# The feed-forward of an encoder layer moved into a phase of its own and computed by one level of Strassen's scheme

## The chip, the cores and the metric

The kernel runs on one core of a Trainium2 chip. Its engines are TensorE (PE, matrix products, with its weight loads listed as PEld), VectorE (DVE), ScalarE (ACT), GpSimd (POOL) and SyncE (SP); SP, ACT and POOL issue the DMAs. The metric is the time of one execution on the device in microseconds (us), the median of several; lower is better.

## What is computed

One layer of a hybrid streaming encoder over 2096 columns (16 meta tokens, 2048 prompt frames, 32 frames of a running stream) of width 1024, all in float32. The change touches the last two lines:

```python
proj = rmsnorm(x) @ w_in                         # 1024 -> 4096: x_a, x_b, g_a, g_b
merged = sig(g_a) * (rglru(conv4(x_a)) @ w_br_a) + sig(g_b) * (pool(x_b) @ w_br_b)
x = x + merged @ w_out                           # "x1" below
g, u = split(rmsnorm(x) @ w_gu)                  # 1024 -> 2 * 2816
y = rmsnorm(x + (silu(g) * u) @ w_down)          # 2816 -> 1024, then the final norm
```

## The kernel before

Data lie with the 1024 features on partitions, in KT = 8 tiles of 128, and frames along the free dimension. The frames go through in NB = 5 blocks of 416 columns (432 in block 0). Every float32 product is made of three passes: each operand is split into a rounded part (hi) and the rest (lo), and `product` (L403 to L406) issues hi x hi, hi x lo and lo x hi, so that one 128x128 piece of weights against one tile of data is three matmuls of 416 columns.

A block runs through the mixer and then the feed-forward. `pe_order` lists the mixer as jobs of 24 matmuls (8 tiles x 3): `xa` (8 jobs), then four rounds p of gates (12 matmuls from the small ring `sring`) with `ga` and `gb` jobs, then `a`, `xb`, two more `gb`, `b` and `o` (x1 = x + o). In block 0 four `fuse` steps of 24 matmuls with 512 columns stand between `xa` jobs. The feed-forward has 22 tiles of hidden features in 11 pairs: for each pair two `g` and two `u` jobs (96 matmuls) and then `dn` (8 outputs x 2 x 3 = 48 matmuls), one pair behind; in all (96 + 48) x 11 = 1584 matmuls a block.

Weights stream from HBM: SP loads 512 KB (1024 columns) into one of RAW = 3 slots `wraw`, ACT writes the hi part into a slot of `wring` (`split_hi`, L553), DVE the lo part (`split_lo`, L1131), and PE uses the slot for one job. The ring has RING = 4 slots. Each engine's order is written out by hand: the calls named `ahead` put ACT's split four slots and DVE's split three slots ahead of the job beside which they stand. PE writes job n into PSUM bank n mod 8, and the reader of the bank (ACT or DVE) frees it.

In the feed-forward DVE and ACT handle each hidden tile in `hidden` (L1101, L744, L748: scale by the norm, Silu, times u, hi and lo parts) and DVE adds each `dn` output to `main` (`add_down`, L1122). The square sums, norm and scaling of the next block's input (`square`, `square_sum`, `invert`, `normalize`) also lie in the feed-forward. In the mixer rounds ACT runs sigmoid, tanh, exp and sqrt, and DVE the scan (`heads`). GpSimd copies small state columns and issues the loads of x and the stores of y. The end of the program (L440 to L450, L1285 to L1291) is a last norm done with small matmuls, eight scalings and the stores.

Of the kernel before, what the change touches and what calls it, by code (L numbers as in the profile page):

```python
# [5 lines left out]
P = 128  # L6
# [3 lines left out]
NB = 5  # L10
# [5 lines left out]
COLS = 2096  # L16
W = 432
# [5 lines left out]
PART = (0, 128, 256, LW - P)  # L23
# [20 lines left out]
def pe_order(b):  # L44
# [14 lines left out]
    for p in range(4 if b else 0):  # L59
        if p == 3:  # L60
            out.append(("n3", b - 1, 0))
# [3 lines left out]
    out += [("xb", b, k) for k in range(KT)]  # L65
# [3 lines left out]
    for i in range(PAIRS + 1):  # L69
        if i < PAIRS:  # L70
            for j in range(2):
                out += [("g", b, 2 * i + j), ("u", b, 2 * i + j)]
                if i == j == 0:
                    out.append(("n2", b, 0))
        if i:
            out += [("dn", b, (i - 1) * KT + m) for m in range(KT)]
        if i == 4 and b < NB - 1:
            out.append(("n1", b + 1, 0))
    if b == NB - 1:
        out.append(("n3", b, 0))  # L80
# [3 lines left out]
ORDER = [name for b in range(NB) for name in pe_order(b)]  # L84
JOB = {name: n for n, name in enumerate(ORDER)}


def slot_order():


    out = []
    for s, b, i in ORDER:
        if s == "dn" and i % 4 == 0:
            out.append(("d", b, i // 4))
        elif s == "w" and i % 4 == 0:
# [33 lines left out]
def side_before():  # L129
# [22 lines left out]
def build(nc, dx, dwm, dws, dcst, dfix, dst0, dy, dst, fused):  # L152
# [4 lines left out]
    MUL, ADD, SUB = ALU.mult, ALU.add, ALU.subtract  # L157
    ctx = ExitStack()
# [1197 lines left out]
```

## Time and profile before

| | before |
|---|---|
| median of 3 runs | 2878.49 us (2877.73 to 2879.58) |
| span of the profiled execution, first to last instruction | 2875.3 us |
| PE busy | 2853.1 us, 15028 matmuls |
| PEld busy | 2821.2 us |
| DVE busy | 1941.4 us, 2843 instructions |
| ACT busy | 1257.3 us, 1762 instructions |
| POOL busy | 98.5 us |
| DMA | 354.5 MB, 123 GB/s |
| mean granted clock of TensorE | 0.998 of full |

Busy is the time in which an engine works on some instruction. Matmuls are pipelined, so the busy time of PE says only that it was fed; how fast it goes is read from the distance between starts. The chain that ended last is the list of work, followed back from the last instruction, in which each piece waits for the one before it.

### The profile page before, as it was taken

Reading aid. Unit: us, or ns where it says so; the run is one execution under the profiler, and the core shown is the slowest. Engines: PE = TensorE matmul, PEld = TensorE weight load, DVE = VectorE, ACT = ScalarE, POOL = GpSimd, SP = SyncE. Lnnn points to the kernel's source line nnn. Section 1 sums busy time; section 2 is a strip of 40 time slices with the busy share of each in tenths; the row PEclk is TensorE's granted clock in tenths of the full one; section 3 lists DMA queues with packets and bytes.
Section 4 is the critical chain, followed back from the end, with each engine's and each line's share of the span. In section 5 each row is a group of like instructions: output and inputs, shape, how many; then the busy total and the mean of one; then the engine's idle time right before and its main releaser. Section 6 shows DMA issues by size and latency. Waiting matters only on the chain.

```text
span 2875.3 us, 37697 instructions
## 1 busy us (share of the span) xinstructions
PE 2853.1 (99%) x15028; PEld 2821.2 (98%) x15028; DVE 1941.4 (68%) x2843; ACT 1257.3 (44%) x1762; POOL 98.5 (3%) x188
## 2 busy tenths in 40 slices
PE   8999999999999999999999999999999999999998
PEld 7999999999999999999999999999999999999998
DVE  7867667677666675776666767766666586766565
ACT  6733434258333433573333336634333275343222
POOL 2000000010000000200000001000000010000000
PEclk9999999999999999999999999999999999999999
DMA  7333333333443333243433332433333324333332
GB/s 244 121 125 126 133 117 111 124 110 110 144 137 124 110 121 117 102 137 134 138 117 117 115 118 102 141 128 127 118 124 117 110 100 146 116 110 125 117 118 78
DMA packets 108188, 354.50 MB, mean 123 GB/s; under 512 B 12144, under 2 KB 22768, under 8 KB 108016
## 3 DMA queue, kind: packets, MB, share of 16 engines
q1 hardware_dynamic: 102624, 336.21, 33.7%
q0 software_dynamic: 4096, 13.64, 1.4%
q8 instruction: 120, 1.97, 0.3%
q10 hardware_dynamic: 1296, 2.26, 0.2%
q14 instruction: 52, 0.43, 0.0%
HBM read 339.19 MB, written 12.87 MB: 122 GB/s over the span
## 4 chain that ended last, share of the span: by engine, by line
PE 98%; DMA 1%; DVE 1%; ACT 0%; issue 0%; SPq 0%; DVEq 0%; ACTq 0%
PE ps L405 97%; DMA wraw<-dwm 1%; SPq L279 0%; DVE gb L941 0%; DMA xres<-dx 0%; DVE main L1291 0%; ACT wring L553 0%; PE ps L432 0%; DVE wring L1131 0%; PE ps L433 0%; ACT sring L559 0%; PE ps L450 0%; DVE ylo L946 0%; ACT main L664 0%; DVE sring L1135 0%
## 5 line engine op out<-in xcount | busy, mean ns | idle before, releaser
L405 PE MATMUL ps<-yhi,wring 128*128 128x416 f32 x4800 | 1309.0, 351 | 0.0
L1131 DVE TENSOR_TENSOR wring<-wraw,wring 128x1024 fp32r<-128x1024 f32 x610 | 746.0, 1224 | 302.2 <-ACT wring L553 301.0
L405 PEld LDWEIGHTS ps<-yhi,wring 128*128 128x128 f32 x4800 | 900.7, 188 | 6.8
L405 PE MATMUL ps<-xhi,wring 128*128 128x416 f32 (+1 forms) x3200 | 875.2, 353 | 8.5 <-DVE wring L1131 8.5
L553 ACT ACTIVATE wring<-wraw 128x1024 fp32r<-128x1024 f32 x610 | 641.0, 1051 | 465.5 <-PE ps L405 460.7
L405 PE MATMUL ps<-ylo,wring 128*128 128x416 f32 x2400 | 841.1, 350 | 0.0
L405 PEld LDWEIGHTS ps<-xhi,wring 128*128 128x128 f32 x3200 | 602.2, 188 | 15.0 <-issue 8.5
L405 PE MATMUL ps<-xlo,wring 128*128 128x416 f32 (+1 forms) x1600 | 562.7, 352 | 0.0
L405 PE MATMUL ps<-hhi,wring 128*128 128x416 f32 x1760 | 485.0, 352 | 0.0
L405 PEld LDWEIGHTS ps<-ylo,wring 128*128 128x128 f32 x2400 | 452.2, 188 | 3.7
L405 PEld LDWEIGHTS ps<-hhi,wring 128*128 128x128 f32 x1760 | 329.3, 188 | 2.4
L405 PE MATMUL ps<-hlo,wring 128*128 128x416 f32 x880 | 307.8, 350 | 0.0
L405 PEld LDWEIGHTS ps<-xlo,wring 128*128 128x128 f32 x1600 | 302.2, 189 | 3.4
L1122 DVE TENSOR_TENSOR main<-ps,main 128x416 f32<-128x416 f32 x440 | 239.7, 585 | 28.7 <-PE ps L405 27.5
L744 ACT ACTIVATE tmp<-tmp 128x416 f32<-128x416 f32 x110 | 60.7, 551 | 310.7 <-DVE tmp L1107 310.7
L748 ACT ACTIVATE hhi<-tmp 128x416 fp32r<-128x416 f32 x110 | 60.7, 552 | 308.6 <-DVE tmp L1113 308.6
L405 PEld LDWEIGHTS ps<-hlo,wring 128*128 128x128 f32 x880 | 165.3, 188 | 2.5
L1107 DVE TENSOR_TENSOR tmp<-ps,rstd_n 128x416 f32<-128x416 f32 x110 | 64.7, 588 | 93.2 <-PE ps L405 93.0
L1115 DVE TENSOR_TENSOR hlo<-tmp,hhi 128x416 fp32r<-128x416 f32 x110 | 65.1, 592 | 67.9 <-ACT hhi L748 67.9
L1113 DVE TENSOR_TENSOR tmp<-ps,tmp 128x416 f32<-128x416 f32 x110 | 65.2, 593 | 49.6 <-PE ps L405 47.9
L941 DVE SCALAR_TENSOR_TENSOR gb<-tbuf,cst,gb 128x416 f32<-128x416 f32 (+3 forms) x144 | 80.2, 583 | 9.2 <-ACT gb L608 5.1
L838 ACT ACTIVATE xhi<-ga 128x416 fp32r<-128x416 f32 x40 | 22.1, 552 | 124.2 <-DVE ga L1241 124.2
(171 smaller groups left out, 1603.8 us busy)
## 6 DMA issues: line engine op xcount, KB each, us to landing
wraw<-dwm SPq DMA_DIRECT2D x577, 512.0 KB, 3.2
wraw<-fused SPq DMA_DIRECT2D x40, 512.0 KB, 3.2
xres<-dx POOLq DMA_DIRECT2D x32, 208.0 KB, 3.0
dy<-main POOLq DMA_DIRECT2D x32, 208.0 KB, 2.2
sraw<-dws SPq DMA_DIRECT2D x24, 256.0 KB, 4.3
fused<-main SPq DMA_DIRECT2D x16, 256.0 KB, 4.1
xres<-dx SPq DMA_DIRECT2D x4, 216.0 KB, 5.4
xres<-dx ACTq DMA_DIRECT2D x4, 216.0 KB, 5.8
```

What stands on the lines that cost most here:

```text
L405: mm = nc.tensor.matmul(out, wt[:, c * P:(c + 1) * P], x, start=(first and q == 0), stop=(last and q == 2))
L553: A(wring[:, n % RING, 0, :], wraw[:, n % RAW, :], ACT.Copy, scale=cst[:, PSC, i:i + 1] if s == "w" else 1.0).then_inc(w_hi, 1)
L744: A(tmp[:, f % 2, 0:LW], tmp[:, f % 2, 0:LW], ACT.Silu).then_inc(silu, 1)
L748: A(hhi[:, f % 4, 0:LW], tmp[:, 2 + f % 2, 0:LW], ACT.Copy).then_inc(h_hi, 1)
L838: A(xhi[:, m, live(b)], ga[:, m, :], ACT.Copy).then_inc(m_hi, 1)
L941: V.scalar_tensor_tensor(gb[:, h, c:c + n], t[:, o + v:o + v + n], cst[:, CW0 + v, h:h + 1], gb[:, h, c:c + n], MUL, ADD).then_inc(tap, 1)
L1107: V.tensor_tensor(t, bank(("g", b, f))[:, 0:LW], rstd[1][:, 0:LW], MUL).then_inc(drained[JOB[("g", b, f)] % 8], 1)
L1113: V.tensor_tensor(h, bank(("u", b, f))[:, 0:LW], t, MUL).then_inc(drained[JOB[("u", b, f)] % 8], 1)
L1115: V.tensor_tensor(hlo[:, f % 4, 0:LW], h, hhi[:, f % 4, 0:LW].bitcast(f32), SUB).then_inc(h_lo, 1)
L1122: V.tensor_tensor(main[:, m, :], bank(name)[:, 0:LW], main[:, m, :], ADD).then_inc(drained[JOB[name] % 8], 1)
L1131: V.tensor_tensor(wring[:, n % RING, 1, :], wraw[:, n % RAW, :], wring[:, n % RING, 0, :].bitcast(f32), SUB).then_inc(w_lo, 1)
```

## The change

The five blocks now run the mixer alone, one after the other. Each leaves x1 in HBM (`x1s`) and, once its norm is known, the normed and scaled y = x1 * rstd * g2 (`ys`, in `make_y`). Then the feed-forward runs as a phase of its own over NT = 3 steps s of 2 x 348 or 2 x 346 columns.

A product of (1024 -> n) on two column halves is cut into 2 x 2 blocks of features and columns, and the Winograd form of Strassen's scheme makes it of 7 half-size products instead of 8. Sums of weight blocks are made on the chip: 34 pieces of weights (4 x 512 columns) are loaded by GpSimd, summed in place by four DVE additions each (`prepare`) and stored in HBM, during blocks 1 to 4. Sums of data blocks are made by three GpSimd subtractions for each of four tile pairs (`operand`), split into hi and lo by ACT and DVE (`operand_hi`, `operand_lo`), before each step s. Partial products that several outputs share are chained in PSUM: two banks (a pair, for gate and up, or for two output tiles) are held through several products, and what has built up is read out in between (`tap_out` by ACT, `add_out` and `add_down` by DVE). A hidden pair p is `gate_up(s, p)`: 7 products k of 24 matmuls, of 348 or 346 columns. `down(s, g)` takes two pairs at once (the last group one): 14 half products hh of 12 matmuls (6 in the last group), each read out by one `add_down` of 2 x 348 columns. The steps are gu0, gu1, gu2, dn0, gu3, gu4, dn1 ... gu9, gu10, dn4, dn5.

To make room the ring has 3 slots (`RING`), so each `ahead` of the same place now handles a slot one earlier. The norm of the next block moves into the stages `a`, `xb` and `o`. The final norm of step s runs in gu0 to gu2 of step s + 1; that of the last step at the end, with a full-width reciprocal in place of the small matmuls.

In the core of the diff below stand, in this order, constants, TensorE's `gate_up`, the sixth product in VectorE's `gate_up`, its `add_down` and `prepare`, and GpSimd's first subtraction in `operand`.

```diff
-RING = 4
+RING = 3
+NT = 3
+TH = (348, 346, 346)
+PROD = (1, 5, 6, 3, 7, 2, 4)
+ROLE = {1: 0, 6: 0, 7: 0, 4: 0, 5: 1, 3: 1, 2: 2}
+REBUILD = {2: 0, 3: 1, 5: 2, 6: 3}
...
+            def gate_up(s, p):
+                for k, prod in enumerate(PROD):
+                    wh, wl = weights(SLOT[("gu", s, p, k)])
...
+                    hold(("gu", s, p, 0, k, 0))
+                    for v in range(2):
+                        out = bank(("gu", s, p, 0, k, v))[:, 0:TH[s]]
+                        for j in range(4):
+                            mm = product(out, wh, wl, 4 * v + j, ycomb[:, c, 0, j, 0:TH[s]], ycomb[:, c, 1, j, 0:TH[s]],
+                                         j == 0 and prod in OPENS, j == 3 and prod in ENDS, True)
+                        mm.then_inc(ready, 1)
...
+                    elif k == 5:
+                        add_out(s, p, 5, 0, 0)
+                        dve.wait_ge(*clear(gu(s, p, 5)))
+                        dve.wait_ge(silu3, n + 1)
+                        V.tensor_tensor(work[:, 7:10, 0:w], work[:, 7:10, 0:w], work[:, 0:3, 0:w], MUL).then_inc(h_mult, 1)
...
+            def add_down(s, g, hh):
...
+                done(name)
...
+                V.tensor_tensor(out, both(name, w), out, ADD).then_inc(cleared[BANK[name] // 2], 1)
...
+            def prepare(b, c):
...
+                V.tensor_tensor(q3, q2, q3, ADD).then_inc(prep_step, 1)
+                dve.wait_ge(prep_step, 4 * i + 1)
+                V.tensor_tensor(q2, q0, q2, SUB).then_inc(prep_step, 1)
+                V.tensor_tensor(q0, q3, q0, SUB).then_inc(prep_step, 1)
+                dve.wait_ge(prep_step, 4 * i + 3)
+                V.tensor_tensor(q1, q1, q0, SUB).then_inc(prep_step, 1)
...
+                if j:
+                    pool.wait_ge(a_lo, 4 * n)
+                nc.gpsimd.tensor_tensor(work[:, 3:5, 0:w], work[:, b0 + 1:b0 + 3, 0:w], work[:, b0:b0 + 2, 0:w], SUB).then_inc(y_diff, 1)
```

The first place is VectorE at the end of a hidden pair and the start of the down products. Before, the pair's last tile is followed by two groups of four additions of one bank (`main<-ps`):

```order
L1110 TENSOR_TENSOR tmp<-tmp,rstd_n 128x416 [waits silu]
L1113 TENSOR_TENSOR tmp<-ps,tmp 128x416 [waits ready,sr_done]
L1115 TENSOR_TENSOR hlo<-tmp,hhi 128x416 [waits h_hi]
L1131 TENSOR_TENSOR wring<-wraw,wring 128x1024 [waits w_hi]
L1122 TENSOR_TENSOR main<-ps,main 128x416 [waits ready] x4
```

Now this stands there, in step 0 from product k = 5 of pair 2 on to the first two additions of dn0 (`xacc<-ps`):

```order
L1503 TENSOR_TENSOR work<-ps,work 128x2x348 [waits cleared0,ready]
L1545 TENSOR_TENSOR work<-work 128x1044 [waits silu3,cleared2]
L1547 TENSOR_TENSOR work<-work 128x696 [waits h_mult]
L1549 TENSOR_TENSOR work<-work 128x348 [waits h_diff]
L1590 TENSOR_TENSOR wring<-wraw,wring 128x1024 [waits w_hi]
L1551 TENSOR_TENSOR hcomb<-work,hcomb 128x696 [waits h_hi]
L1555 TENSOR_TENSOR work<-ps,work 128x348 [waits cleared0,ready]
L1558 TENSOR_TENSOR work<-work 128x348 [waits h_diff,cleared0]
L1560 TENSOR_TENSOR hcomb<-work,hcomb 128x1044 [waits h_hi]
...
L1563 TENSOR_TENSOR hcomb<-work,hcomb 128x348 [waits h_hi]
L1565 TENSOR_TENSOR hcomb<-work,hcomb 128x348 [waits h_hi]
L1579 TENSOR_TENSOR xacc<-ps,xacc 128x2x348 [waits x1_in,ready]
```

The whole work of a pair (three products' worth of hidden data) comes after its sixth and seventh product, and the additions of dn come behind it. On TensorE the products of that place wait for pairs of banks. `cleared0` to `cleared3` are the four pairs; the last two products of pair 2 and the first three of dn0 are:

```order
L635 MATMUL ps<-ycomb,wring 128x348 [waits cleared2,w_lo]
L635 MATMUL ps<-ycomb,wring 128x348 x23
L635 MATMUL ps<-ycomb,wring 128x348 [waits cleared0,w_lo]
L635 MATMUL ps<-ycomb,wring 128x348 x23
L635 MATMUL ps<-hcomb,wring 128x348 [waits w_lo,cleared3,h_lo,h_hi]
L635 MATMUL ps<-hcomb,wring 128x348 x11
L635 MATMUL ps<-hcomb,wring 128x348 [waits cleared0,w_lo]
L635 MATMUL ps<-hcomb,wring 128x348 x11
L635 MATMUL ps<-hcomb,wring 128x348 [waits cleared3,w_lo]
```

Before, a dn job stood in one of eight banks in turn, six matmuls each. Now the second half product of dn takes the pair that the seventh product of the hidden pair has just left (cleared by L1555), and the third adds onto what the first left (read by the first L1579).

The third place is ScalarE in dn4, where the data sums of the next step are split (`ycomb<-work`, the waits `y_diff` are for GpSimd's subtractions) between the weight splits (`wring<-wraw`) of the running products:

```order
L795 ACTIVATE wring<-wraw 128x1024 [waits ready,raw_in1]
L1004 ACTIVATE ycomb<-work 128x2x346 [waits y_in0,ready]
L1005 ACTIVATE ycomb<-work 128x346
L1007 ACTIVATE ycomb<-work 128x3x346 [waits y_diff]
L1009 ACTIVATE ycomb<-work 128x346 [waits y_diff]
L795 ACTIVATE wring<-wraw 128x1024 [waits ready,raw_in2]
L1004 ACTIVATE ycomb<-work 128x2x346 [waits y_in1,ready]
```

Before, nothing of the kind stood in the feed-forward; ScalarE had there, for each hidden tile:

```order
L744 ACTIVATE tmp<-tmp 128x416 [waits drained4]
L553 ACTIVATE wring<-wraw 128x1024 [waits ready,raw_in1]
L748 ACTIVATE hhi<-tmp 128x416 [waits drained5]
L553 ACTIVATE wring<-wraw 128x1024 [waits ready,raw_in2]
```

## Rows read from the trace of the kernel before

**Rows 1.** The page: busy time of the engines, and the chain by engine.
```profile
PE 2853.1 (99%) x15028; PEld 2821.2 (98%) x15028; DVE 1941.4 (68%) x2843; ACT 1257.3 (44%) x1762; POOL 98.5 (3%) x188
PE 98%; DMA 1%; DVE 1%; ACT 0%; issue 0%; SPq 0%; DVEq 0%; ACTq 0%
```

**Rows 2.** Waits of PE, the longest: us in total, times, longest.
```profile
PE ps L405 <- DVE wring L1131: 8.5, 1, 8.5
```

**Rows 3.** The chain in order of time: start us, us, what; two steady stretches.
```profile
315.19 118.03 PE ps L405 x624
694.93 183.88 PE ps L405 x972
```

**Rows 4.** Timeline of PE: start us, us, line, operation, shapes, count.
```profile
45.39 4.28 PE L405 MATMUL ps<-wring,sring 128*128 128x512 f32 x18
...
51.98 0.56 PE L405 MATMUL ps<-xhi,wring 128*128 128x432 f32 x2
...
55.50 0.55 PE L405 MATMUL ps<-xhi,wring 128*128 128x432 f32 x2
...
2863.29 0.35 PE L445 MATMUL ps<-ones,tot 128*128 128x2 f32 x2 [1.36 <-ACT sq L577]
2863.51 0.36 PE L446 MATMUL ps<-ones,sq 128*128 128x2 f32 x2
```

**Rows 5.** Timeline of PE, last matmul, and DVE and ACT behind it.
```profile
2861.58 0.35 PE L405 MATMUL ps<-hhi,wring 128*128 128x416 f32 x1
2861.97 0.59 DVE L1122 TENSOR_TENSOR main<-ps,main 128x416 f32<-128x416 f32 x1
...
2862.60 0.55 ACT L577 ACTIVATE sq<-main 128x416 f32<-128x416 f32 x1 [0.58 <-DVE main L1122]
```

**Rows 6.** Groups by form: busy us, mean ns of one | idle before, releaser.
```profile
L1131 DVE TENSOR_TENSOR wring<-wraw,wring 128x1024 fp32r<-128x1024 f32 x610 | 746.0, 1224 | 302.2 <-ACT wring L553 301.0
L553 ACT ACTIVATE wring<-wraw 128x1024 fp32r<-128x1024 f32 x610 | 641.0, 1051 | 465.5 <-PE ps L405 460.7 <-DMA wraw<-dwm 4.7
...
L1122 DVE TENSOR_TENSOR main<-ps,main 128x416 f32<-128x416 f32 x440 | 239.7, 585 | 28.7 <-PE ps L405 27.5
...
L744 ACT ACTIVATE tmp<-tmp 128x416 f32<-128x416 f32 x110 | 60.7, 551 | 310.7 <-DVE tmp L1107 310.7
...
L901 DVE RECIPROCAL rstd_n<-rstd_n 128x416 f32<-128x416 f32 x13 | 35.7, 2750 | 36.1 <-ACT rstd_n L587 36.1
```

**Rows 7.** Timeline of DVE at the start of block 0: weight splits, square sums between.
```profile
12.80 2.37 DVE L1131 TENSOR_TENSOR wring<-wraw,wring 128x1024 fp32r<-128x1024 f32 x2
...
21.59 2.47 DVE L1128 SCALAR_TENSOR_TENSOR wring<-wraw,cst,wring 128x1024 fp32r<-128x1024 f32 x2
```

**Rows 8.** Timeline of block 1's rounds: first gates on PE, two splits on DVE.
```profile
642.21 0.35 PE L405 MATMUL ps<-yhi,sring 128*128 128x416 f32 x1
...
654.16 1.22 DVE L1131 TENSOR_TENSOR wring<-wraw,wring 128x1024 fp32r<-128x1024 f32 x1
...
676.55 1.22 DVE L1131 TENSOR_TENSOR wring<-wraw,wring 128x1024 fp32r<-128x1024 f32 x1
```

**Rows 9.** Windows: stretch, us, busy PE PEld DVE ACT POOL, clock, DMA share, GB/s.
```profile
305.70:605.90 300.20, 300.20 (x1590) 297.69 (x1589) 192.87 (x266) 106.99 (x136) 1.61 (x3) 1.00 0.33 117
...
642.00:715.40 73.40, 73.40 (x390) 72.85 (x389) 52.93 (x79) 65.71 (x98) 0.19 (x1) 1.00 0.31 104
```

**Rows 10.** Timeline of PE at the one long wait of block 0.
```profile
84.28 0.73 PE L405 MATMUL ps<-yhi,sring 128*128 128x432 f32 x1 [2.76 <-ACT tmp L676]
84.81 0.56 PE L405 MATMUL ps<-ylo,sring 128*128 128x432 f32 x1
```

**Rows 11.** Windows, columns as in rows 9: the same place.
```profile
84.00:88.00 4.00, 3.72 (x12) 3.54 (x13) 1.60 (x3) 4.00 (x9) 0.00 (x0) 0.59 0.00 0
```

**Rows 12.** Timeline of POOL: subtractions and products on 8 columns, early and later.
```profile
14.17 1.06 POOL L332 TENSOR_TENSOR lac<-lac 128x8 f32<-128x8 f32 x1
...
27.52 0.20 POOL L341 TENSOR_TENSOR lac<-lac 128x8 f32<-128x8 f32 x1
```

**Rows 13.** DMA issues: KB each, median us from issue to landing.
```profile
xres<-dx POOLq DMA_DIRECT2D x32, 208.0 KB, 3.0
```

More of the change, by code:

```diff
@@ L64, in pe_order @@
     out += [("a", b, m) for m in range(KT)]
-    out += [("xb", b, k) for k in range(KT)]
+    for k in range(KT):
+        out.append(("xb", b, k))
+        if k == 1 and b < NB - 1:
+            out.append(("n1", b + 1, 0))
     out += [("gb", b, 6), ("gb", b, 7)]
@@ L398, in free, with hold, product, full @@
             def free(name):
-                n = JOB[name]
-                if n >= 8:
-                    pe.wait_ge(drained[n % 8], n // 8)
-            def product(out, wh, wl, c, xh, xl, first, last):
+                if len(name) == 3 and NEED[name]:
+                    pe.wait_ge(drained[BANK[name]], NEED[name])
+            def hold(name):
+                if NEED[name]:
+                    pe.wait_ge(cleared[BANK[name] // 2], NEED[name])
+                else:
+                    for q in range(2):
+                        pe.wait_ge(drained[BANK[name] + q], MIXED[BANK[name] + q])
+            def product(out, wh, wl, c, xh, xl, first, last, chain=False):
                 for q, (wt, x) in enumerate(((wh, xh), (wh, xl), (wl, xh))):
-                    mm = nc.tensor.matmul(out, wt[:, c * P:(c + 1) * P], x, start=(first and q == 0), stop=(last and q == 2))
+                    mm = nc.tensor.matmul(out, wt[:, c * P:(c + 1) * P], x, start=(first and q == 0), stop=(last and q == 2), skip_group_check=chain)
                 return mm
-            def full(name, xh, xl, before=()):
+            def full(name, xh, xl, before=(), cols=None):
                 s, b, i = name
@@ L418, in full, with column_sum @@
                 mm.then_inc(ready, 1)
[L420 to L423 removed]
+            def column_sum(name):
+                kind, b, _ = name
+                if name == ("n1", 0, 0):
                     pe.wait_ge(sq_summed, sq_index(kind, b, 7) + 1)
                     free(name)
[L426 removed]
+                    nc.tensor.matmul(bank(name)[:, 0:W], ones[:].bitcast(f32), tot[:, 0:W], start=True, stop=True).then_inc(ready, 1)
@@ new lines, in down @@
+            def down(s, g):
+                n, width = s * PAIRS + GROUPS[g][-1] + 1, len(GROUPS[g])
+                pe.wait_ge(h_hi, 4 * n)
+                pe.wait_ge(h_lo, 4 * n)
+                for hh in range(14):
+                    mp, k = divmod(hh, 7)
+                    wh, wl = weights(SLOT[("dn", s, g, hh // 2)])
+                    c = COMBO[PROD[k]]
+                    hold(("dn", s, g, mp, k, 0))
+                    for v in range(2):
+                        out = bank(("dn", s, g, mp, k, v))[:, 0:TH[s]]
+                        for t, p in enumerate(GROUPS[g]):
+                            mm = product(out, wh, wl, 2 * width * (hh % 2) + width * v + t, hcomb[:, p % 3, 0, c, 0:TH[s]],
+                                         hcomb[:, p % 3, 1, c, 0:TH[s]], t == 0 and PROD[k] in OPENS, t == width - 1 and PROD[k] in ENDS, True)
+                        mm.then_inc(ready, 1)
```

986 lines of the change are left out of this document (661 added, 325 removed).

## The prediction

> **What bounds the kernel now.** I read the page first: PE is busy 99% of the span and 98% of the chain is PE [rows 1]. Then the waits: the longest of PE is 8.5 us, once, at the start [rows 2]. So nothing but TensorE sets the time, and every other engine is cover. The chain in order of time says how fast PE goes: 624 matmuls in 118.03 us and 972 in 183.88 us, 189.2 ns from start to start at 416 columns [rows 3]. The timeline gives the same for other widths: six times three matmuls of 432 columns from 51.98 to 55.50 are 195.6 ns each, and 18 of 512 columns in 4.28 us, less 0.36 to 0.40 for the last one's own length, are 228 to 231 ns [rows 4]. That is a slope of about 0.41 ns a column and some 19 ns that do not shrink. Two matmuls of 2 columns with their weight loads start 0.22 us after the two before, 110 ns each [rows 4]. So loading weights does not hold the rate at 346 columns either, and fewer columns do pay.
>
> **The products.** Before, 1584 matmuls x 5 blocks = 7920 x 189.2 ns = 1498.5 us; the window over one feed-forward has 300.2 us for it [rows 9]. After, each step s has 11 x 168 (gate and up) + 84 x 11 (down) = 2772 matmuls. At 0.41 ns a column the one step of 348 columns has 161.3 ns, the two of 346 have 160.5 ns: 2772 x 161.3 + 5544 x 160.5 = 1337 us. **Gain 161 us**, not the 187 us (an eighth) that the count of columns gives, since 396 more matmuls each carry the fixed part. Column sums change by less than 1 us.
>
> The fixed part is where a page can be weighed. In the Trainium skill, "TensorE: Matmul & The Clock Gate", Part 2, the gap between matmuls is N/2.4 + 2.5 ns at full clock. By that 416 columns are 175.8 ns, 13 ns below the rows, and the gain would be 7920 x 175.8 - 8316 x about 147 = 170 us; I keep the rows.
>
> **What the cover must now do, a hidden pair.** Seven products of 24 matmuls are 3.86 us each, 27.0 us a pair. VectorE has 0.585 us at 416 and 1.224 at 1024 columns [rows 6], so 0.51, 0.88 and 1.25 us at 348, 696 and 1044; a second one behind an independent first comes 0.09 earlier (two splits in 2.37) [rows 7]. ScalarE has 0.55 and 1.05 us at 416 and 1024 [rows 6]. A matmul's end is 0.35 us after its start, 0.16 later than the next could start, and an engine that waits starts 0.04 after it [rows 5]. A pair's sum on VectorE (7 splits, 3 additions of two banks, and the hidden work) is 18 us of 27: enough. The order is what matters. From the end R of the sixth product's slot: 0.16 + 0.04, addition of two banks 0.88, Silu on 1044 columns 1.1, product 1.29, differences 0.92 and 0.55, split 1.13, lo part 0.79, seventh product's multiply 0.42 = 7.3 us. The pair of banks that this last step frees is wanted again at R + 7.7 where another hidden pair follows: 0.35 us of slack, no wait (18 places). Two-bank and strided forms are in no row; priced as one wide one at the low end, and 0.1 more each at the high end.
>
> **Hidden pair to down.** Where dn follows, the half products are 1.93 us, and that bank pair is wanted at R + 3.86 + 1.93 = 5.8: PE waits 1.6. The third half product adds onto the first, so it needs VectorE's first addition, and that stands behind difference, lo part, split and two more lo parts and itself: 7.3 + 4.5 = 11.8 us after R, wanted at 7.7. PE comes out **4.1 us late**, and nothing gives it back. 15 such places; 13 plain ones cost 53 us. Behind that the additions (2 x 0.79 + 1.13 = 2.7 us in 3.86) keep up. In dn5 (6 matmuls, 0.96 us) they don't: 2 x 0.79 + 0.6 = 2.2 us against 1.93 a slot, 2 us each time; the first dn of steps 1 and 2 also waits for the residual, loaded only after the y stores of gu2: 1 to 2 us each. One dn5 and both of these are 5 us (two dn5 stand below).
>
> **Rebuilding the data sums.** In dn4 of steps 0 and 1 four operands go one after another through a load (3.0 us to land [rows 13]), three subtractions on POOL, the hi parts on ACT, the lo parts on DVE (each waits for the former's lo parts), and ACT's and DVE's weight splits and additions are queued behind these waits. POOL on hundreds of columns is in no row. On 8 columns it takes 0.20 us, and 1.06 where DVE is at work [rows 12]; with VectorE's slope on top, an operand is 2.0 us at the low end, and 6.1 us with contention and a doubled slope. Walking the order with these, dn5 begins its third half product 14 to 24 us late; I take 18 (DVE is busy 7 tenths of the time, nearer the contended row): 36 us for both, the 4.1 inside. The same chain in the last `o` stage, four operands in 36 us with the last one started at the sixth job, makes the first hidden pair 7 us late (5 to 10).
>
> The Trainium skill, "SBUF — State Buffer", § SBUF: two separate sides, says that GpSimd and VectorE instructions with two SBUF inputs lock each other out for a whole instruction. That agrees with 1.06 against 0.20, and it would make VectorE wait too; it is a rival below.
>
> **The ring of 3.** In the rounds of block 1 gates start at 642.2 [rows 8], so with 2.27 us for gates and 4.54 a job gb0 starts at 653.5. The split at 654.16 is for the slot one earlier now, gb0's: done at 655.4, 1.9 us late. The one at 676.55 serves gb2, wanted at 674.0: 1.8 more. The other splits of the rounds end before they are wanted on the delayed schedule. 3.7 x 4 = 15 us. The sums of weights (34 x 2.75 us on DVE) lie in its idle time: it is busy 52.9 of 73.4 us there [rows 9], and they come after the splits; if a load is late they cost up to 10 us. In block 0 the split at 21.59 [rows 7] is now slot 2, wanted at 19.6: 3.2 us late; the fuse steps, two slots each out of three, and the first quad add some 7: 10 us (3 to 20).
>
> **The end.** Before, the last matmul ends at 2861.9 and the span at 2875.3: 13.4 us. Now: last addition 0.9, six sums of squares of 0.93, split 1.7, sums 1.3, root 0.8, a reciprocal of 692 columns (2.75 us at 416 [rows 6]) 4.6, eight scalings 6.9, store 2.1 = 24; with three sums in dn5: +12.
>
> **The clock.** After a wait of 2.76 us matmuls of 432 columns come 0.36 us apart instead of 0.195, and the granted clock is 0.59 over those 4 us: 1.2 GHz for ten matmuls, 1.65 us lost [rows 10, 11]. Waits of 1.4 us cost nothing of the kind. The 2.6 us at each dn are near the former; I take half of 15 x 1.65 = 12 us, from 0 to 25.
>
> **Sum**: -161 + 53 + 36 + 5 + 7 + 15 + 10 + 12 + 12 = -11. The profiled span of 2875.3 becomes 2864, and the median lies 3.2 above the span: **2867 us**, 0.4% faster: nine tenths of the gain is given back. Its own range is 2835 to 2900.
>
> **Rivals.**
> *The tails are covered.* If the additions of dn come in time, the 53 and 12 go, and half of the 36: 2867 - 83 = 2784. For it: VectorE's sum is far below PE's. Against: the order of the instructions, in which no addition can pass the hidden work.
> *The slack of 0.35 us is none.* A chain of nine steps over three engines, four of them in forms that no row shows; with 0.15 us more for each, 1.0 us is lost at 18 places between hidden pairs and 1.3 more at 15 dn, 38 us, and the clock falls at most of them (+30): 2935. It decides from 0.35 us on; this is the case slower than before. Against it: all hand-offs in the rows are 0.04 us.
> *The lock.* If VectorE waits for GpSimd as well, twelve subtractions of 1.3 us stop it in each rebuild and at the entry, some 8 us each on the path: 2891. By the skill's rule named above.
> *It doesn't do what it says*: PE held by weight loads would leave 8316 x 189.2, 75 us more; rows 4 exclude it.
>
> **Chances.** Forecast 0.5 (of that 0.28 under 2872.7, 0.12 within 0.2%, 0.10 above), tails covered 0.27, no slack 0.18, lock 0.05. What a measurement can tell is about 0.2%, 5.8 us. Faster 0.55, same 0.13, slower 0.32. The range reaches from the covered case to most of the slower one: 2780 to 2925.
>
> **What would show it.** On the chain steady PE stretches at 160 to 161 ns in the hidden pairs; in PE's waits some 15 times 1.6 and 2.6 us for VectorE (`work<-ps`, `xacc<-ps`); two larger heaps at dn5 for ACT or DVE; granted clock below 1 at dn. A share of PE waits below 40 us, or waits between hidden pairs, makes the forecast wrong.

## The result

| | before | after |
|---|---|---|
| median | 2878.11 us (2877.53 to 2879.58) | 2899.27 us (2897.45 to 2899.66) |
| profiled span | 2875.3 us | 2897.4 us |
| PE busy, matmuls | 2853.1 us, 15028 | 2720.9 us, 15404 |
| DVE busy | 1941.4 us | 2104.6 us |
| DMA | 354.5 MB, 123 GB/s | 481.87 MB, 166 GB/s |
| granted clock of TensorE | 0.998 | 0.981 |

The changed kernel is **slower by 0.73%** (ratio 1.0073, interval 1.0059 to 1.0088). The forecast was 2867 us, 0.4% faster. The time lies just inside the range given for that sum (2835 to 2900); the direction is the other one.

The page, busy time and the chain by engine, as in [rows 1]:

```profile
PE 2720.9 (94%) x15404; PEld 2676.2 (92%) x15404; DVE 2104.6 (73%) x2784; ACT 1367.3 (47%) x1849; POOL 250.6 (9%) x425
PE 67%; DVE 15%; ACT 7%; issue 5%; DMA 2%; POOL 2%; SPq 0%; DVEq 0%; ACTq 0%; POOLq 0%
```

PE's waits (us in total, times, longest); before, only the one of 8.5 us was longer than 3 us [rows 2]:

```profile
PE ps L635 <- DVE xacc L1579: 65.8, 33, 5.3
PE ps L635 <- DVE work L1555: 33.6, 19, 3.2
PE ps L635 <- DVE wring L1590: 30.2, 21, 8.7
PE ps L635 <- issue: 14.0, 1, 14.0
PE ps L673 <- issue: 8.5, 1, 8.5
PE ps L635 <- DVE xlo L1256: 5.2, 4, 1.3
```

PE is busy for 132 us less and waits instead, mostly for VectorE: PE's share of the chain falls from 98% to 67%. Between the first and the last instruction 154 us more are idle than before (2897.4 - 2720.9 against 2875.3 - 2853.1).

The windows show where (stretch, us, then busy time with counts of PE, PEld, DVE, ACT, POOL, clock, DMA share, GB/s). The first two are two hidden pairs of step 0 and of step 1, 336 matmuls each. The next two are dn4 with dn5 in steps 0 and 1, where the data operands are rebuilt, and the fifth is the same in step 2, where nothing is rebuilt, up to the last product.

```profile
1527.63:1581.12 53.49, 53.49 (x339) 53.49 (x338) 29.75 (x31) 24.19 (x29) 0.00 (x0) 1.00 0.42 137
2105.05:2158.33 53.28, 53.28 (x338) 53.28 (x338) 29.69 (x31) 24.15 (x29) 0.00 (x0) 1.00 0.42 138
1838.23:1902.02 63.79, 45.87 (x255) 42.99 (x253) 53.71 (x66) 24.39 (x34) 24.30 (x24) 0.92 0.41 131
2328.48:2392.56 64.08, 47.42 (x255) 44.77 (x254) 53.34 (x66) 24.47 (x34) 24.16 (x24) 0.89 0.41 131
2824.02:2871.40 47.38, 42.26 (x253) 39.65 (x252) 39.90 (x50) 16.34 (x22) 0.00 (x0) 1.00 0.22 73
```

In the hidden pairs PE never waits: 53.49 / 336 = 159.2 ns and 53.28 / 336 = 158.6 ns a matmul. The rebuilds last 16.4 and 16.7 us longer than the same place in step 2.

Next, PE's timeline at dn0 of step 0 and at dn2 of step 0, then the windows behind each second wait.

```profile
1494.83 2.07 PE L635 MATMUL ps<-hcomb,wring 128*128 128x348 f32 x12
1498.54 2.14 PE L635 MATMUL ps<-hcomb,wring 128*128 128x348 f32 x12 [1.64 <-DVE work L1555]
1503.04 7.20 PE L635 MATMUL ps<-hcomb,wring 128*128 128x348 f32 x34 [2.37 <-DVE xacc L1579]
...
1671.07 2.15 PE L635 MATMUL ps<-hcomb,wring 128*128 128x348 f32 x12 [1.61 <-DVE work L1555]
1675.57 4.70 PE L635 MATMUL ps<-hcomb,wring 128*128 128x348 f32 x28 [2.36 <-DVE xacc L1579]
```

```profile
1503.00:1507.00 4.00, 3.96 (x16) 3.99 (x17) 2.67 (x3) 0.00 (x0) 0.00 (x0) 0.62 0.51 152
1676.00:1680.00 4.00, 4.00 (x27) 4.00 (x26) 2.56 (x4) 0.27 (x1) 0.00 (x0) 1.00 0.50 164
```

The two waits of the forecast are there, 1.6 and 2.4 us. Behind the first pair of them the granted clock is at its lower level, 1.2 GHz, for 3.4 us (16 matmuls start in 4 us); below this is called a fall of the clock. Behind the second, with the same waits, it stays at 2.4 GHz (27 matmuls).

And VectorE at the same dn0 of step 0, from the last addition of the hidden pair on, in the order that the part on the change shows:

```profile
1491.21 0.88 DVE L1503 TENSOR_TENSOR work<-ps,work 128x696 f32<-128x696 f32 x1 [1.44 <-PE ps L635]
1493.31 1.25 DVE L1545 TENSOR_TENSOR work<-work 128x1044 f32<-128x1044 f32 x1 [1.21 <-ACT work L1056]
...
1495.95 1.22 DVE L1590 TENSOR_TENSOR wring<-wraw,wring 128x1024 fp32r<-128x1024 f32 x1
1497.09 0.88 DVE L1551 TENSOR_TENSOR hcomb<-work,hcomb 128x696 fp32r<-128x696 f32 x1
1497.88 0.51 DVE L1555 TENSOR_TENSOR work<-ps,work 128x348 f32<-128x348 f32 x1
...
1502.02 1.67 DVE L1579 TENSOR_TENSOR xacc<-ps,xacc 128x696 f32<-128x696 f32 x2
```

With R = 1491.0, the end of the sixth product's slot, L1555 ends at R + 7.4 and the first L1579 starts at R + 11.0 and ends near R + 11.9: what the forecast walked out (7.3 and 11.8).

### The profile page after: what moved, and what is told of

Read it like the earlier page. It is cut to its first block, busy times and chain, and to the rows that moved or that the text cites. A ratio compares the mean times of both kernels' runs of the same rounds, so it can differ in the third digit from the quotient of the medians.

```text
span 2897.4 us, 39533 instructions
## 1 busy us (share of the span) xinstructions
PE 2720.9 (94%) x15404; PEld 2676.2 (92%) x15404; DVE 2104.6 (73%) x2784; ACT 1367.3 (47%) x1849; POOL 250.6 (9%) x425
## 2 busy tenths in 40 slices
DMA packets 166729, 481.87 MB, mean 166 GB/s; under 512 B 18800, under 2 KB 41840, under 8 KB 166544
## 3 DMA queue, kind: packets, MB, share of 16 engines
q0 software_dynamic: 31664, 117.66, 11.8%
## 4 chain that ended last, share of the span: by engine, by line
PE 67%; DVE 15%; ACT 7%; issue 5%; DMA 2%; POOL 2%; SPq 0%; DVEq 0%; ACTq 0%; POOLq 0%
PE ps L635 67%; DVE wring L1590 2%; ACT wring L795 2%; DVE xacc L1579 1%; DMA work<-ys 1%; DVE tmp L1336 1%; DVE work L1545 1%; DVE gb L1305 1%; DVE tmp L1439 1%; POOL work L557 1%; ACT work L1056 1%; DVE main L1721 1%; DVE tmp L1252 1%; DVE xlo L1256 1%; ACT L896 1%
## 5 line engine op out<-in xcount | busy, mean ns | idle before, releaser
L1590 DVE TENSOR_TENSOR wring<-wraw,wring 128x1024 fp32r<-128x1024 f32 (+1 forms) x637 | 768.1, 1206 | 298.8 <-ACT wring L795 296.6
L795 ACT ACTIVATE wring<-wraw 128x1024 fp32r<-128x1024 f32 (+1 forms) x637 | 661.6, 1039 | 620.1 <-PE ps L635 616.6
L635 PE MATMUL ps<-ycomb,wring 128*128 128x346 f32 (+1 forms) x5544 | 890.7, 322 | 23.3 <-issue 14.0
L635 PEld LDWEIGHTS ps<-ycomb,wring 128*128 128x128 f32 x5544 | 887.3, 190 | 25.0 <-issue 25.0
L635 PE MATMUL ps<-hcomb,wring 128*128 128x346 f32 (+1 forms) x2772 | 477.2, 333 | 90.9 <-DVE xacc L1579 65.8
L635 PEld LDWEIGHTS ps<-hcomb,wring 128*128 128x128 f32 x2772 | 461.3, 197 | 104.8 <-issue 82.4
L635 PE MATMUL ps<-yhi,wring 128*128 128x416 f32 x1280 | 347.1, 351 | 2.6 <-DVE wring L1590 2.6
L1579 DVE TENSOR_TENSOR xacc<-ps,xacc 128x692 f32<-128x692 f32 (+1 forms) x252 | 218.3, 877 | 94.4 <-PE ps L635 90.8
L635 PEld LDWEIGHTS ps<-yhi,wring 128*128 128x128 f32 x1280 | 240.2, 188 | 4.8 <-DVE wring L1590 3.2
L635 PE MATMUL ps<-ylo,wring 128*128 128x416 f32 x640 | 224.5, 351 | 0.0
L1503 DVE TENSOR_TENSOR work<-ps,work 128x692 f32<-128x692 f32 (+1 forms) x99 | 87.1, 880 | 105.0 <-PE ps L635 105.0
L635 PEld LDWEIGHTS ps<-ylo,wring 128*128 128x128 f32 x640 | 120.0, 188 | 1.4
```

Source lines behind the costliest of these rows:

```text
L635: mm = nc.tensor.matmul(out, wt[:, c * P:(c + 1) * P], x, start=(first and q == 0), stop=(last and q == 2), skip_group_check=chain)
L795: A(wring[:, n % RING, 0, 0:c], wraw[:, n % RAW, 0:c], ACT.Copy, scale=cst[:, PSC, name[2]:name[2] + 1] if name[0] == "w" else 1.0).then_i ...
L1503: V.tensor_tensor(c, both(name, TH[s]), c, ADD).then_inc(cleared[BANK[name] // 2], 1)
L1579: V.tensor_tensor(out, both(name, w), out, ADD).then_inc(cleared[BANK[name] // 2], 1)
L1590: V.tensor_tensor(wring[:, n % RING, 1, 0:c], wraw[:, n % RAW, 0:c], wring[:, n % RING, 0, 0:c].bitcast(f32), SUB).then_inc(w_lo, 1)
```

## The experiments

Two questions were open: is it the order of VectorE's instructions or their amount, and what do the clock, the ring of 3 and the rebuilds cost each. Places are compared by the time from a stage's first matmul to the next stage's first. The excess of a stage is this time less what its matmuls take at the steady 159.2 or 158.6 ns. Each run's trace is of one execution, so differences of one or two microseconds between two traces can be chance. The diffs shown are against the changed kernel; three dots stand for lines left out.

### The order at the end of a hidden pair (e1_tail)

VectorE, with what stands now between the addition L1503 of product k = 5 and the third addition of dn:

```diff
                         add_out(s, p, 5, 0, 0)
+                        split_lo(SLOT[("gu", s, p, 6)] + RING - 1)
                         dve.wait_ge(*clear(gu(s, p, 5)))
                         dve.wait_ge(silu3, n + 1)
...
-                dve.wait_ge(h_hi, 4 * n + 1)
-                V.tensor_tensor(hl[:, 0:2, :], work[:, 7:10:2, 0:w], hh[:, 0:2, :].bitcast(f32), SUB).then_inc(h_lo, 1)
                 name = gu(s, p, 6)
                 done(name)
                 dve.wait_ge(*clear(name))
                 V.tensor_tensor(work[:, 10, 0:w], bank(name)[:, 0:w], work[:, 6, 0:w], MUL).then_inc(cleared[BANK[name] // 2], 1)
...
                         add_down(s, i, hh)
+                        if after_gu(s, "dn", i):
+                            at = STEPS[STEPS.index(("dn", i)) - 1][1]
+                            if hh % 2:
+                                split_lo(SLOT[("dn", s, i, hh // 2)] + RING - 1)
+                            if hh in LATER[i]:
+                                for q in LATER[i][hh]:
+                                    rest(s, at, q)
```

The last multiply (L1555) now stands ahead of the lo parts. `rest` holds the four last instructions of the hidden pair (L1558 to L1565), and `LATER` puts them behind some of the additions, mostly one at a time. ScalarE's weight splits stand ahead of its waits in the same manner.

> The changed kernel with VectorE's and ScalarE's instructions at the end of a hidden pair in another order, none left out: the weight split of the sixth product before the wait for Silu, the seventh product's multiply (L1555) before the lo parts, and at dn the additions of the half products between what is left of the hidden work. Theory ORDER: PE's waits at dn (15 places of 1.6 + 2.4 us, 4.4 with the restart) and at the second hidden pair of each step (3 of 2.9 to 3.2) come only from what stands ahead in VectorE's queue; they go, and with them most of the clock's loss behind them (some 20 us by the excess of the slow stages): 2899 - 66 - 10 - 20 = 2803 us (2785 to 2825), PE waits for work<-ps and xacc<-ps under 10 us outside the two rebuilds. Rival AMOUNT: VectorE has too much to do at dn (25.3 us busy of 32.7 us), so the waits only move to later half products: 2885 to 2900 us.

Measured: **2838.54 us**, ratio to before 0.9859 (0.9843 to 0.9876). The same place of PE:

```profile
1490.74 1.27 PE L636 MATMUL ps<-ycomb,wring 128*128 128x348 f32 x7
1491.85 8.42 PE L636 MATMUL ps<-hcomb,wring 128*128 128x348 f32 x52
```

No wait is left. Of the 15 dn that follow a hidden pair, 11 have neither a rebuild nor a late residual behind them: dn0 to dn3 of step 0, dn1 to dn3 of step 1, dn1 to dn4 of step 2. There the excess falls from 59 us to 0.5, and at the first hidden pairs with the column sums behind them from 17 to 5 us. No instruction was taken away, so it was the order and not the amount: theory ORDER. The size was 35 us too good and the time outside the range (2785 to 2825), since other waits grew: dn4 and dn5 of steps 0 and 1 lose 54 us instead of 48, and dn0 of steps 1 and 2 now waits 6.6 and 6.8 us for the residual instead of 4.4 and 6.9 in two parts.

### PE's idle time filled (e2_busy)

```diff
+                    if g < 5 and hh in (1, 2):
+                        keep_busy(("dn", s, g, 0, 5, 0), hcomb[:, GROUPS[g][0] % 3, 0, 0, 0:160], 17 if hh == 1 else 25)
                     hold(("dn", s, g, mp, k, 0))
```

`keep_busy` issues so many matmuls of 160 columns into columns that nobody reads; 30 more stand ahead of the second hidden pair of each step.

> The changed kernel with matmuls of 160 columns, whose result nobody reads, in PE's idle time: 17 ahead of the second and 25 ahead of the third half product of dn0 to dn4, 30 ahead of the second hidden pair of each step. Nothing else is moved, all waits stay. Theory CLOCK: idle time of PE lets the granted clock fall and that costs about 1.55 us at 9 of 13 plain dn places, more in dn4, and 4.3 us at two of the three second pairs: with PE kept busy 2899 - 14 - 4 - 2 = 2879 us (2874 to 2885), clock 0.99. Rival: the clock does not follow PE's idle time, or the matmuls that fill it are too slow: 2899 us or up to 10 more, clock 0.98.

Measured: **2887.58 us**, 12 us less than the changed kernel, clock 0.988. Windows over dn0 of step 0, the changed kernel and then e2_busy (columns as above):

```profile
1494.83:1527.63 32.80, 28.79 (x171) 28.28 (x170) 25.31 (x29) 9.98 (x11) 0.00 (x0) 0.95 0.35 114
```

```profile
1493.41:1524.90 31.49, 31.49 (x213) 31.49 (x211) 25.29 (x29) 10.00 (x11) 0.00 (x0) 1.00 0.37 119
```

At seven plain dn where the clock had fallen the stage is 1.1 to 1.3 us shorter and the clock 1.00, and where it had not fallen the stage is 0.2 us longer, the price of the extra matmuls. The two pairs behind the column sums where it had fallen gain 1.5 and 2.5 us. So at these places a fall costs 1.3 to 1.5 us and follows from the idle time: theory CLOCK. Dn0 of step 1 is 3.5 us longer (the clock is low there for 6.8 us instead of 3.4), and the rebuilds gained nothing (0.7 us more together), so 12 us came of the expected 20, outside the range (2874 to 2885). The profiled execution is the slowest of the five (2890.13), so its stages add up to 9 us.

### The additions alone (e8_adds)

```diff
+                        late = after_gu(s, "dn", i) and hh < 4
...
+                        if late:
+                            for q in {0: (0,), 1: (1,), 2: (2, 3)}.get(hh, ()):
+                                rest(s, STEPS[STEPS.index(("dn", i)) - 1][1], q)
```

Here `rest` is L1560, the weight split, L1563 and L1565; L1555 is not moved.

> The changed kernel with nothing moved but VectorE's additions of the first half products of dn: the first stands ahead of the lo part L1560, the second ahead of the weight split, the third behind it. L1555, which frees the pair of banks for the second half product, stays where it is. Theory TWO WAITS: the 1.6 us (for work<-ps) stays at all 15 places, the 2.4 us (for xacc<-ps) goes, and with it the clock's fall, which at dn always came behind the second wait: at 11 plain places 2.6 us each, at 8 of them 1.5 us more, 2899 - 29 - 12 = 2858 us (2850 to 2868), as dn0 of steps 1 and 2 and dn4 wait for something else next. Rival: without the second the third addition is late by as much, and the clock falls behind the 1.6 us alone: 2885 to 2899 us.

Measured: **2872.01 us**, ratio to before 0.9983 (0.9973 to 0.9992). At dn0 of step 0:

```profile
1493.21 2.07 PE L635 MATMUL ps<-hcomb,wring 128*128 128x348 f32 x12
1496.91 9.35 PE L635 MATMUL ps<-hcomb,wring 128*128 128x348 f32 x57 [1.64 <-DVE work L1555]
```

At the 11 plain places the 1.6 us stays, the 2.4 us is gone, and the clock is 1.00 at each: theory TWO WAITS in its mechanism. The time is 4 us above its range (2850 to 2868). Each such dn is 2.2 us shorter where the clock had held and 3.5 to 3.8 where it had fallen, 36 us with the 1.9 of dn0 of step 1. Of that 8 us are lost again elsewhere: dn4 and dn5 of the rebuilds 4.4 us, dn0 of step 2 1.0 us, and the pair behind the sums of step 1, where the clock falls now and did not before, 2.7 us.

### The ring of 3 slots alone (e3_ring3)

The kernel before with `RING = 3`, and with what hangs on it fitted: the first weight splits at the start, and the loads of `sring` one slot earlier, as in the changed kernel.

> The kernel before with RING = 3 instead of 4 and nothing else. Theory RING: the mixer's stages lose what they lose in the changed kernel, 7 to 9 us in block 0 and 3.3 to 5.4 us in each round stage of blocks 1 to 4: 2878 + 9 + 16 = 2903 us, less what block 0 has for other reasons (2895 to 2908); the xa stages of blocks 1 to 4 do not change. Rival SUMS: the losses come from the weight sums and the norm work that the change put into the mixer: within 5 us of 2878.

Measured: **2916.98 us**, ratio 1.0138 (1.0123 to 1.0153). Of the 38.8 us in the span, 32.8 lie in the mixer; the changed kernel's mixer lost 32.0 us up to the last `o`:

| us more than before | block 0 | xa, blocks 1 to 4 | rounds, blocks 1 to 4 | rest |
|---|---|---|---|---|
| changed kernel | 8.9 | 6.0 | 16.4 | 0.7 |
| before with 3 slots | 5.5 | 8.9 | 18.4 | 0.0 |

So the ring accounts for the mixer's loss, but for some 3.5 us in xb and the gb behind it in block 0, and xa belongs to it, against what was expected; with that the time is 9 us above the range (2895 to 2908). The other 6 us lie in the feed-forwards of the old form, 1.0 to 1.4 us each.

### The weight sums (e6_sums8)

> The changed kernel with the weight sums (prepare, L1259 to L1274) on 8 columns instead of 512 or 1024: the sums are left out but for these, loads, stores and waits stay, so the output is another. Theory HIDDEN: VectorE does them in idle time, except for some 1.6 us in the rounds and 1.2 us in xb of block 2, where there are nine instead of eight: 2899 - 3 = 2896 us (2893 to 2900). Rival: they, and not the ring of 3 slots, hold up the weight splits of the rounds and of xa: 2899 - 16 to 22 = 2877 to 2883.

Measured: **2903.19 us**: no gain, 4 us more, and outside the range (2893 to 2900). The rounds of blocks 1, 3 and 4 did not move by 0.5 us. The two places that lost are block 0 (2.7 us) and the second round of block 2 (1.6 us), each with one more fall of the clock than in the changed kernel's trace; why is not shown. VectorE's 94 us of weight sums (34 x 2.75) cost nothing, as the forecast had it. The short instructions and their waits for the loads are still there, so this says nothing of the loads.

### No rebuilding (e9_norebuild)

> The changed kernel without the data operands of steps 1 and 2: their loads, GpSimd's subtractions and the hi and lo parts are left out, and these steps compute with the operands of step 0, so the output is another. Theory LOAD: dn4 and dn5 of steps 0 and 1 then last as in step 2, where nothing is rebuilt: 39.5 + 24.3 and 40.1 + 24.0 us become 31.1 to 32.7 + 16.3 each: 2899 - 32 = 2867 us (2860 to 2873), which is the price of both rebuilds, clock and all, and the 4.4 us at dn4 stay. Rival: the waits there come from dn5's short half products and the residual and not from the operands: 2885 to 2895 us.

Measured: **2867.45 us**, 31.8 us less: theory LOAD. Dn4 and dn5 of step 0 last 31.3 and 16.9 us instead of 39.5 and 24.3. This is the price of both rebuilds, 16 us each, clock and all.

### Loads ahead, and subtractions on VectorE (e4_both, e5_dvesub)

```diff
-TAKE = {2: 0, 4: 1, 6: 2, 7: 3}
+TAKE = {1: 0, 3: 1, 5: 2, 7: 3}
...
+            def operand(s, j):
+                n, w, b0 = 4 * s + j, TH[s], y_base(j)
                 if j:
                     pool.wait_ge(a_lo, 4 * n)
+                    fetch(s, j + 1)
+                pool.wait_ge(y_in[j % 2], 48 * (n // 2 + 1))
```

`fetch` issues the three loads of an operand. At the start of the phase `TAKE` also moves three of the four splits of operands one `o` tile forward, which the expectation doesn't name.

> e1_tail, and GpSimd issues the loads of a data operand ahead of the subtractions of the one before (and the first two before the stage o or the end of the last hidden pair). Theory LATENCY: the 14.0 us at the start of the feed-forward phase is four times a chain of issue (1.6), landing (3 to 4), subtractions (5) and splits; with the loads hidden it falls to 0 to 3 us, and the two rebuilds lose 5 to 10 us each less: e1_tail - 15 - 15 = some 30 us below e1_tail. Rival LOAD: VectorE is the bound there (54 us of work for 40 us of PE in dn4 and dn5), so the rebuilds keep 17 us or more each, and only the start gains: e1_tail - 14.

Measured: **2827.52 us**, 11 us below e1_tail. The wait at the start falls from 14.2 to 10.0 us, and dn4 with dn5 from 54 to 46 us of excess. Of the 30 us of LATENCY a third came; the size is nearer to LOAD's 14, and the rebuilds keep 23 us each, but they gained more than the start did. How much of the 4 us at the start is the loads' and how much that of `TAKE` is not shown. VectorE and GpSimd in dn4 of step 0 show what remains:

```profile
1818.70 3.21 DVE L1615 TENSOR_TENSOR wring<-wraw,wring 128x1024 fp32r<-128x1024 f32 x1
1821.83 1.59 DVE L1475 TENSOR_TENSOR ycomb<-work,ycomb 128x692 fp32r<-128x692 f32 x1
1823.35 1.23 DVE L1477 TENSOR_TENSOR ycomb<-work,ycomb 128x346 fp32r<-128x346 f32 x1
```

```profile
1819.13 1.69 POOL L561 TENSOR_TENSOR work<-work 128x692 f32<-128x692 f32 x1
1820.90 1.79 POOL L563 TENSOR_TENSOR work<-work 128x346 f32<-128x346 f32 x1
1822.76 1.44 POOL L565 TENSOR_TENSOR work<-work 128x346 f32<-128x346 f32 x1
```

The weight split takes 3.21 us where it has 1.22 alone, and spans one GpSimd subtraction wholly; the next two take 0.7 us more each. The split reads and writes other data than the subtractions, so it doesn't wait for their results. Then the subtractions went to VectorE (three instructions at the head of `operand_lo`):

> e4_both with the three subtractions of each data operand on VectorE instead of GpSimd, nothing else moved. Theory LOCK: beside GpSimd's subtractions VectorE's weight split took 3.2 to 3.4 us instead of 1.22, and the two first lo parts of an operand 1.6 and 1.24 instead of 0.88 and 0.51, some 3.5 us an operand; its own subtractions cost 0.88 + 0.52 + 0.52 = 1.9 us, so VectorE wins 1.6 us an operand, 6.5 us a rebuild, and 6 to 7 us at the start of the phase: 2827 - 13 - 7 = 2807 us (2798 to 2817), the split back at 1.22. Rival ADDED WORK: VectorE is the bound in dn4 and dn5 and gets 1.9 us more for each of 12 operands while the long instructions only waited where it had time: 2827 + 15 to 23 = 2842 to 2850.

Measured: **2823.77 us** (2823.04 to 2826.47), where e4_both had 2827.52 (2823.49 to 2827.58): 4 us less by the medians, but the ranges overlap, so hardly a gain. Neither theory had the size. The same place:

```profile
1822.68 1.22 DVE L1621 TENSOR_TENSOR wring<-wraw,wring 128x1024 fp32r<-128x1024 f32 x1
1823.82 0.88 DVE L1475 TENSOR_TENSOR work<-work 128x692 f32<-128x692 f32 x1
...
1825.72 0.87 DVE L1481 TENSOR_TENSOR ycomb<-work,ycomb 128x692 fp32r<-128x692 f32 x1
1826.51 0.51 DVE L1483 TENSOR_TENSOR ycomb<-work,ycomb 128x346 fp32r<-128x346 f32 x1
```

Every duration is back, so it was GpSimd's subtractions that stretched VectorE's instructions. The size of LOCK failed for a reason that the traces show. The split is stretched to 3.2 to 3.4 us at four of the 12 operands and not at each. Over the whole trace of e4_both the stretching adds up to some 23 us (an estimate: what VectorE's instructions near a subtraction take above their usual time), and VectorE's own subtractions (12 times 0.88 + 0.52 + 0.52) cost 23 us. The windows over dn4 and dn5 of step 0, in e4_both and then in e5_dvesub, show it in little:

```profile
1806.21:1869.72 63.51, 47.86 (x255) 45.51 (x253) 58.42 (x65) 24.06 (x34) 23.59 (x21) 0.87 0.38 120
```

```profile
1810.20:1871.50 61.30, 47.38 (x254) 44.86 (x253) 57.08 (x77) 23.79 (x34) 5.42 (x9) 0.86 0.39 124
```

In both VectorE is busy for over nine tenths of a rebuild (58.42 of 63.51 us, 57.08 of 61.30). Of the kernels here only e9_norebuild takes that away: 40.44 of 48.12 us. The Trainium skill, "SBUF — State Buffer", § SBUF: two separate sides, has the rule: a VectorE instruction with two SBUF inputs and a GpSimd one that reads SBUF lock each other out of a shared pair of ports, and the one that starts first has it for its whole instruction. The 3.21 against 1.22 us agree with a lock-out; which of the two started first can't be read here, since the spans on POOL are rough.

### A version that beats both (e7_best)

```diff
-                elif p == 1 and 2 <= k <= 4:
-                    finish(s - 1, k - 2)
-                elif p == 2 and k <= 4:
-                    finish(s - 1, k + 3)
+                for i in {(1, 2): (0, 1), (1, 3): (2,), (1, 4): (3,), (1, 5): (4, 5), (2, 1): (6, 7)}.get((p, k), ()) if s else ():
+                    finish(s - 1, i)
...
-TAKE = {2: 0, 4: 1, 6: 2, 7: 3}
+TAKE = {0: 0, 2: 1, 4: 2, 6: 3}
```

All of e5_dvesub is in it too.

> e5_dvesub, and two more moves. The eight scalings of the final norm of steps 0 and 1 stand in the second hidden pair and at the start of the third (six and two instead of three and five), so the residual's load starts some 15 us earlier: theory RESIDUAL: in e4_both the first addition of dn0 in steps 1 and 2 waits 6.4 and 6.7 us for it and with the clock that is 8.8 and 8.2 us: -17 us. And the operands at the start of the phase are split beside o tiles 0, 2, 4, 6 instead of 1, 3, 5, 7: -2 to -4 us. Together e5_dvesub - 19 (-16 to -22), some 2788 us. Rival: the residual's landing is held up by the queue of GpSimd, not by the scalings: 0 to -4 us.

Measured: **2807.04 us** (2805.50 to 2811.91), ratio to before 0.9758 (0.9742 to 0.9775): 2.4% faster than before, 3.2% than the changed kernel. It is 16.7 us below e5_dvesub, inside the 16 to 22 expected; the 2788 rested on a forecast of 2807 for e5_dvesub. The wait for the residual (x1, loaded into `xacc`) falls from 5.2 and 6.8 us to 0.7 and 1.1 and the two dn0 by 14 us, theory RESIDUAL; the last `o` stage and the first hidden pair are 3 us shorter. What is left of PE's waits:

```profile
PE ps L638 <- DVE wring L1619: 33.5, 23, 8.8
PE ps L638 <- DVE xacc L1608: 33.3, 18, 5.5
PE ps L676 <- issue: 8.6, 1, 8.6
PE ps L638 <- DVE xlo L1260: 5.3, 4, 1.3
PE ps L638 <- issue: 5.1, 1, 5.1
```

## Why the forecast was wrong

Each term of the forecast's sum against the trace of the changed kernel (spans, us). The clock is a line of its own, so it is left out of the others; block 0 has one fall before and one after. The entry is the start of the feed-forward phase. The 13 plain dn are the 11 named at e1_tail and dn0 of steps 1 and 2.

| term | forecast | measured | from |
|---|---|---|---|
| products | -161 | -178 | 2772 x 159.2 + 5544 x 158.6 = 1320.6 against 1498.5 |
| 13 plain dn | +53 | +58 | 1.6 + 2.4 and 0.4 for restarting twice |
| two rebuilds | +36 | +38 | 63.8 + 64.1 - 2 x 40.0 = 48, less 10 for the clock (an estimate: five falls, two of them of 6.8 us, at 1.3 to 1.5 us for each 3.4) |
| third dn5, residual | +5 | +6 | 2.9; 0.4 and 2.9 |
| first hidden pair | +7 | +14 | 13.99 |
| rounds with 3 slots | +15 | +16 | 3.8, 5.4, 3.8, 3.3 |
| xa and xb, blocks 1 to 4 | 0 | +7 | 4 x 1.5 and 1.8, less some 0.3 a block |
| pair behind the column sums | 0 | +9 | 3.17 + 2.89 + 2.89 and the sums |
| block 0 | +10 | +9 | |
| end | +12 | +13 | 26.0 against 13.4 |
| clock | +12 | +30 | what is left of the 22.1 |
| **sum** | **-11** | **+22** | |

**What was right.** No wait between plain hidden pairs (18 places forecast, 15 found; the excess there is 0.00 nearly everywhere), so the rival *The slack of 0.35 us is none* falls. At dn the two waits came out at 1.6 and 2.4 us against 1.6 and 2.6. The rebuilds, the end, the rounds and block 0 are within 2 us.

**The products** gained 17 us more than put: the slope of 0.41 ns a column from [rows 4] gave 160.5 and 161.3 ns; the measured 158.6 is (189.2 - 158.6) / 70 = 0.44 ns a column. The Trainium skill, "TensorE: Matmul & The Clock Gate", Part 2, gives the gap at full clock as N/2.4 + 2.5 ns, for a matmul without its weight load. By that formula, an estimate, the gap at 346 columns would be 146.7 ns: 12 ns below the trace, as it was 13 below at 416. So for this stream the formula's time is too short at both widths. Its gain of 170 us lay nearer to the 178 than the rows' 161 all the same, since an error that is nearly alike at both widths mostly drops out of the difference.

**The steps that failed are the clock and three waits of the small stages.** The clock is the largest single term that was mis-sized: put at half of 15 x 1.65 = 12 us, with 25 as its upper end, and 30 in the trace. The price of one fall was right (1.3 to 1.5 us by e2_busy, 1.65 at the place in [rows 10]), their number was not: 18 stretches of slow clock ahead of the last product, where the kernel before has one. Nine are at the 13 plain dn, five in the rebuilds, two behind the column sums, one at the entry and one in block 0. They last 3.4 or 6.8 us, the one at the entry 17 us, most of it in PE's wait there. The forecast had a wait of 2.76 us with its price and took half since 2.6 is "near"; what it didn't count is that the rebuilds, the entry and the residual have longer waits. In the changed kernel a fall goes with each wait of 3.1 us and more, and with one of the two of 2.9 us.

**Three waits were not in the sum or too small**, together 23 us, more than the clock's 18. Each follows from the code that the forecast read. (1) The column sums take a whole pair of banks between the first and second hidden pair of a step, so that the next product wants the pair that L1555 frees at once, not one product (3.8 us) later: some 3 us, 3 times. The waits behind the sums of step 0 and at the entry, on PE:

```profile
1439.30 0.92 PE L635 MATMUL ps<-ycomb,wring 128*128 128x348 f32 x2 [3.17 <-DVE work L1555]
```

```profile
1406.27 1.21 PE L635 MATMUL ps<-ycomb,wring 128*128 128x348 f32 x3 [13.99 <-issue]
```

In the 18 places without a wait these three were counted in. (2) The ring of 3 also holds up the start of xa, 1.5 us a block; the forecast walked the rounds alone. e3_ring3 shows it as the ring's (2.2 us a block there). (3) At the entry an operand took 10.5 to 11.5 us from load to load (issue 1.6, landing 2.9 to 4.0, GpSimd 4.3 to 5.3, and the x1 stores in its queue), and the chain of four ended 14 us late instead of 7. Of this one only a part was tested: e4_both and e7_best bring the wait to 10.0 and 5.1 us.

With the products 17 us better, the clock 18 worse, these three 9 + 7 + 7 worse, and the small terms together 9, the sum goes from -11 to +22. The forecast also put the median 3.2 us above the span; in the runs it is 1.9 to 2.3 us. Without the clock's 18 us the sum would stand at +4, without the 23 us of the three waits at -1: only both together make up the distance.

**The lock** was priced as a case of its own (2891, chance 0.05). It was real but small: in the changed kernel VectorE's instructions beside GpSimd's subtractions are stretched by some 11 us in all, 6 at the entry and 5 in the rebuilds, whose 36 us had been sized by the contended row [rows 12]. Taking it away in e5_dvesub gave next to nothing. It was not what set the sign. **The tails are covered** (2784) did not come about, but e1_tail shows that they can be at the 11 plain dn, by order alone. The argument against it, that "no addition can pass the hidden work", holds for the order as it was written and for no other.

**Open**: why the clock falls at seven of the 11 plain dn, whose waits are alike to 0.05 us. (The other two of the nine falls have a second wait of 2.8 and 5.3 us.) e8_adds says that there the 1.6 us alone never brings it about. Elsewhere single waits hardly longer did: 1.86 us in block 0 of the changed kernel, and 1.78 us in block 2 of e1_tail, while the changed kernel has the same 1.78 us at that place without a fall. So the length of a wait alone doesn't decide it below 3 us.

## What to carry over

When an engine that was always fed is given short waits, count every wait, those of the small stages too, and put the full price of the slow clock on each that is as long as one behind which a trace shows a fall, pairs of short waits with little work between them included; here the clock cost half of what the waits at the 13 plain dn did. Where a buffer is freed by the last step of a long chain, the order of the engine's queue says when it comes free, and not the engine's share of busy time: moving instructions that TensorE waits for ahead of others that nobody waits for was worth 61 us, and taking away 94 us of work elsewhere on the same engine nothing. Where a change adds a holder of banks (the column sums here), walk the rotation once more through each place where it stands.

## What the runs showed of the chip

- VectorE's 1024-wide split of 1.22 us takes 3.18 to 3.43 us at four places beside GpSimd's subtractions (e4_both), and a 348-wide lo part 1.25 instead of 0.51 (the changed kernel), though they share no data.
- GpSimd's subtraction on 692 or 696 columns takes 1.65 to 2.5 us and on 346 or 348 columns 0.92 to 1.97 us (the changed kernel); VectorE needs 0.88 and 0.52 us for the same (e5_dvesub).
- Matmuls of 160 columns with their weight loads came 110 ns apart (25 in 2.75 us, e2_busy), the same as two of 2 columns [rows 4]: between these widths the width made no difference.
- A two-bank addition from PSUM of 2 x 346 columns takes 0.88 us, as much as an SBUF one of 692.
- The granted clock fell behind two waits of 1.6 and 2.4 us, with 2.1 us of matmuls between them, at seven of 11 places, and cost 1.3 to 1.5 us each time; short matmuls in the idle time kept it at 2.4 GHz at all 11 (e2_busy).
